# A sparse-expert stage whose first two experts get their token rows separately

## The reference

```
g_idx = argmax(h @ w_group + b_group)                  # one of 4 groups
el    = (h @ w_expert).reshape(N, 4, 8)[group] + b_expert
vals, idx = top_k(softmax(el), 2)                      # two experts of a token
for each expert e, over the rows of its tokens:
    y = (silu(x @ w1[e]) * (x @ w3[e])) @ w2[e]        # 1024 -> 512 -> 1024
out[token] += y * weight
```

## Time and profile before

| | us |
|---|---|
| median of 3 runs | 1858.24 (1854.73, 1858.24, 1860.97) |
| profiled execution, own time | 1859.26 |
| its span, first to last instruction | 1857.5 |
| PE busy | 1701.7 (92%) |
| mean granted TensorE clock | 0.978 of full |
| read from HBM | 329.75 MB |

### The profile page before, as it was taken

One profiled execution on the slowest core, in us unless ns is written; L12 is line 12 of the kernel. 1 busy time (PEld: TensorE's weight loads), 2 busy tenths in 40 slices (PEclk: granted clock), 3 DMA queues, 4 the chain that ended last, 5 costly groups with the idle time before them and its releaser, 6 DMA issues.

```text
span 1857.5 us, 24733 instructions
## 1 busy us (share of the span) xinstructions
PE 1701.7 (92%) x10405; PEld 1297.4 (70%) x10405; DVE 712.4 (38%) x1529; ACT 594.9 (32%) x1048; POOL 169.2 (9%) x128
## 2 busy tenths in 40 slices
PE   7999999997998877778889999997999899999998
PEld 5878766886564444444468966766788798888886
DVE  4355345454111111211135567555734532222223
ACT  3434354422011000000134456554624432222222
POOL 1000110221111111101001000011101000000221
PEclk9999899998999999999999999998999999999999
DMA  7512100358899999999994331012420232223201
GB/s 259 182 46 91 47 23 23 122 195 339 350 411 408 410 395 407 404 409 407 427 361 180 94 110 66 1 46 108 176 91 12 91 103 91 91 87 137 93 23 46
DMA packets 79580, 341.90 MB, mean 184 GB/s; under 512 B 8007, under 2 KB 15815, under 8 KB 66024
## 3 DMA queue, kind: packets, MB, share of 16 engines
q1 hardware_dynamic: 73192, 329.76, 46.0%
q0 software_dynamic: 5120, 8.40, 1.4%
q10 hardware_dynamic: 1152, 2.10, 0.3%
HBM read 329.75 MB, written 18.87 MB: 188 GB/s over the span
## 4 chain that ended last, share of the span: by engine, by line
PE 70%; DMA 19%; DVE 5%; ACT 4%; issue 2%; SPq 0%; POOL 0%; DVEq 0%; POOLq 0%; ACTq 0%
PE ps L553 66%; DMA arenaf<-in_w 14%; DMA arenaf<-in_mem 3%; DMA hf<-in_w_xkv 2%; PE ps L972 1%; PE ps L2881 1%; DMA ring<-in_w_in 1%; ACT splitr L629 1%; DVE arenaf L2963 1%; PE ps L807 1%; DVE splitr L618 0%; DVE arenaf L2981 0%; ACT arenaf L961 0%; PE ps L2059 0%; DVE xf L3259 0%
## 5 line engine op out<-in xcount | busy, mean ns | idle before, releaser
L553 PE MATMUL ps<-hr,splitr 128*128 128x512 f32 (+1 forms) x2784 | 579.1, 367 | 6.9 <-POOL hr L904 4.3
L553 PEld LDWEIGHTS ps<-hr,splitr 128*128 128x128 f32 x2784 | 476.5, 193 | 88.9 <-issue 5.1
L553 PE MATMUL ps<-splitr,hr 128*128 128x512 f32 (+1 forms) x1488 | 273.7, 343 | 2.2 <-DVE hr L1069 1.4
L553 PEld LDWEIGHTS ps<-splitr,hr 128*128 128x128 f32 x1488 | 234.2, 189 | 35.8 <-issue 2.0
L618 DVE TENSOR_TENSOR splitr<-ring,splitr 128x2048 fp32r<-128x2048 f32 x61 | 142.9, 2343 | 232.8 <-ACT splitr L629 232.6
L629 ACT CAST splitr<-ring 128x2048 fp32r<-128x2048 f32 x61 | 116.1, 1905 | 152.0 <-PE ps L553 142.7
L2096 DVE SCALAR_TENSOR_TENSOR tq<-ps,arenaf,tq 128x256 f32<-128x256 f32 x32 | 15.5, 484 | 268.8 <-PE ps L553 236.3
L2132 ACT COPY junk<-ps 64x512 f32<-64x512 f32 x32 | 18.5, 578 | 288.8 <-PE ps L553 288.8
L553 PE MATMUL ps<-arenaf,tq 128*64 128x512 f32 x336 | 81.5, 629 | 31.0 <-DMA arenaf<-in_w 31.0
L553 PE MATMUL ps<-arenaf 128*64 128x128 f32 (+7 forms) x784 | 103.0, 342 | 5.5 <-ACT arenaf L979 3.5
L618 DVE TENSOR_TENSOR splitr<-arenaf,splitr 128x2048 fp32r<-128x2048 f32 x27 | 62.2, 2303 | 104.9 <-ACT splitr L629 104.9
(11 more groups left out here) (395 smaller groups left out, 1926.0 us busy)
## 6 DMA issues: line engine op xcount, KB each, us to landing
ring<-in_w SPq DMA_DIRECT2D x22, 2048.0 KB, 43.1
arenaf<-in_w SPq DMA_DIRECT2D x22, 2048.0 KB
splitf<-in_w SPq DMA_DIRECT2D x21, 2048.0 KB, 44.0
hf<-in_w SPq DMA_DIRECT2D x20, 2048.0 KB, 44.5
ring<-in_w_in SPq DMA_DIRECT2D x11, 2048.0 KB, 9.6
otf<-in_w SPq DMA_DIRECT2D x11, 2048.0 KB
ring<-in_w_gate_up SPq DMA_DIRECT2D x7, 2048.0 KB, 7.9
arenaf<-in_w_in SPq DMA_DIRECT2D x4, 2048.0 KB
```

Of the source, the lines that this page charges most:

```text
L553: return te.matmul(out, lhsT, rhs, start=start, stop=stop)
```

## The change

The rows of pair 0 are no longer turned and gained for both experts at once. `pe_first_rows(e)` waits for the rows of expert e alone, and turns 64 rows (8 transposes that give 128x64) into two banks of its own. `ve_first_rows(e)` gains them. Expert 1's step stands behind `pe_up(0)`. Later pairs are as before. The events `("ert", 0, half)`, for which POOL's gathers 4 and 5 wait, now come with expert 1's transposes. `take` is called four times for pair 0 where it was called twice.

```diff
+            def pe_first_rows(e):
+                a = CAP * e
+                for half in range(2):
+                    ps = take("ert", 0, half, e)
+                    for w in pe_at(("rows", e)):
+                        te.wait_ge(*w)
+                    for k in range(4 * half, 4 * half + 4):
+                        c = CAP * (k % 4)
+                        it = te.transpose(ps[:, c:c + CAP], XG[0][a:a + CAP, k:1024:8], ident[a:a + CAP, a:a + CAP])
+                    it.then_inc(*pe_done("rows turned", ("ert", 0, half, e), *([("ert", 0, half)] if e else [])))
+
+            def ve_first_rows(e):
+                for half in range(2):
+                    ks = slice(4 * half, 4 * half + 4)
+                    gain = gain_moe[:, ks].rearrange("p (k o) -> p k o", o=1).broadcast_to([128, 4, CAP])
+                    for w in ve_at(("ert", 0, half, e), ("gain_moe",)):
+                        ve.wait_ge(*w)
+                    ve.tensor_tensor(XTF[:, ks, e, :], thirds(bank("ert", 0, half, e)[:, 0:4 * CAP], 4),
+                                     gain, ALU.mult).then_inc(
+                        *ve_done("rows gained", ("xgain", e, half, "first"), ("free", "ert", 0, half, e),
+                                 *([("xgain", 0, half)] if e else [])))
...
-                        for s in pe_at(("xgain", b // 2, k // 4)):
+                        for s in pe_at(("xgain", b // 2, k // 4) if b > 1 else ("xgain", b, k // 4, "first")):
...
             def pe_experts():
-                pe_rows(0)
+                pe_first_rows(0)
                 for b in range(33):
                     if b < 32:
                         pe_up(b)
+                    if b == 0:
+                        pe_first_rows(1)
...
             def ve_experts():
                 places_ = ve_extra_places()
-                ve_rows(0)
+                ve_first_rows(0)
                 for b in range(33):
                     if b < 32:
                         ve_hidden(b)
+                    if b == 0:
+                        ve_first_rows(1)
```

## The result

| | before | after |
|---|---|---|
| median, us | 1857.95 (6 runs, 1854.73 to 1860.97) | 1865.66 (6 runs, 1861.32 to 1870.72) |
| profiled execution: its own time, span | 1859.26, 1857.5 | 1861.32, 1859.4 |

The ratio is 1.0041, with a 95% interval of 1.0026 to 1.0055. The change made the kernel slower by 7.7 us, with an interval from 4.8 to 10.2. I had predicted +2.05 us. The sign was right, but 1865.66 lies above my range. The same kernel was timed once more later on beside the kernel before, and gave a ratio of 1.0029 (1.0017 to 1.0041), or 4.85 us.

What follows compares the result with a forecast made beforehand. Bound: PE's chain, and in the expert stage a full weight queue whose start follows expert 0's w1 product. Experts -0.95, bank wait +3.0, w_out_2 0: +2.05 on 1858.24 gives 1860.3 us, range 1854.5 to 1864.5.

Steps and rivals of the forecast that it cites:

- The experts: Expert stage: 1.7 us earlier start less 0.75 for gathers 4 and 5, so -0.95 us, between -2.9 and +0.2.
- The wait for gather 0 alone: Before expert 0's first product: PE no longer waits for gather 1, so its transposes start 1.3 us earlier.
- Half the rows: Before the first product: turning 64 rows saves 0.1 us, the smaller first gain 0.27.
- The clock in product 0: Expert 0's first product: the rise from 1.2 to 2.4 GHz follows the work, so the whole 1.7 us stays.
- rival 2: First product: the clock doesn't follow the work, gain only 0.85, experts -0.1, total +2.9, 1861.1 us; chance 0.20.
- rival 3: First product: the clock rises early, product ends 3.6 us earlier, experts -2.9, total +0.1, 1858.3 us; chance 0.09.
- Gathers 4 and 5: Expert stage: both gathers now run inside the full weight queue and cost 0.75 us, 1.07 by their share.
- The bank at the start of the attention: Sparse attention: first scores take mcol's bank and wait 2.6 us for ACT, clock 0.4 more; +3.0 (1.6 to 3.9).
- Rival 1: Start of the sparse attention: the stage swallows the new wait, which costs nothing; total -0.95, 1857.3 us; chance 0.16.
- Rival 4: First part of the attention: the clock stays at 1.2 GHz after the new gap; +4 more, 1864.3 us; chance 0.07.
- The product with w_out_2: Its 0.88 us wait goes, but PE then waits for head 3's squares: 0 us, bound -0.8.

Runs made afterwards that it cites:

- e1: Kernel before plus eight transposes of the identity in the middle of the expert stage; 1864.04 us against 1859.13, ratio 1.0029.
- e3: Kernel after with the bank ring's counter moved on by six at the end of PE's expert list; 1860.57 us against 1859.13 of before, ratio 1.0006.
- e11: Kernel before with the ring moved on by two after PE's expert list and eight identity transposes mid-stage; 1864.56 us against 1858.52, ratio 1.0036.
- e12: Kernel after, word for word, timed again beside the kernel before; 1863.37 us against 1858.52, ratio 1.0029.
- e9: Kernel before plus four transposes of the identity in the middle of the expert stage; 1864.06 us, timed only once.
- e10: Kernel before plus twelve transposes of the identity in the middle of the expert stage; 1863.05 us, timed only once.
- e4: Kernel before with the bank ring's counter moved on by two at the end of PE's expert list; 1861.51 us against 1859.13, ratio 1.0014.
- e5: Kernel before with gathers 4 and 5 also waiting for expert 0's turned hidden values, so as late as in after; 1859.66 us against 1858.47, ratio 1.0009.
- e2: Kernel after plus eight transposes of the identity in the middle of the expert stage; 1862.05 us, ratio 1.0019 to the kernel before.
- e6: Kernel after with the ring moved on by six after PE's expert list and eight identity transposes mid-stage; 1859.19 us against 1858.47 of before, ratio 1.0003.
- e7: e6 with expert 1's rows also turned and gained ahead of the first product; 1859.29 us against 1858.47 of before, ratio 1.0002.
- e8: e6 with gather 4 waiting only for expert 0's transposes and gather 5 for expert 1's; 1858.39 us against 1858.47 of before, ratio 1.0000.

## Why the prediction was wrong

**The step that failed is the list of what the change moves.** The prediction goes through PE's added work as time: eight transposes for 0.3 us that other work hides. As time this is right. What it leaves out is that they are also code. The prediction has no term for the branch, and this is the largest part of the miss: in the five profiles with the whole second pause (after, e1, e3, e11, e12) the stretch "branch" takes 13.56 us in the mean, in the eight without a second pause 10.70 (e9, with a part of the pause, is in neither). That is +2.9 us, and the two groups don't overlap: 12.61 to 14.21 against 9.65 to 11.35.

The pause of 3.73 us behind the branch could be read in the trace of before, and beside it the queue that serves it. It is q8, "instruction", with 84 packets and 1.38 MB in the whole kernel before, and 85 and 1.39 MB after. These are its rows among the DMA queues from 945 to 960 us, of before with three packets and then of e10 with two:

```profile
q8 instruction: 3, 0.05, 1.4%
```

```profile
q8 instruction: 2, 0.03, 0.9%
```

One packet is 16384 bytes. Away from the branch they are 12 to 43 us apart. Behind the branch the first two start at 951.0 and 954.2 before, and at 947.4 and 950.7 after: the second is not asked for until 3.2 or 3.3 us after the first. In the kernel after PE runs again at 949.97, uses up what the first block has left behind the branch's place (two matmuls), and waits until 953.62 for the second. The Trainium skill (Runtime: NRT & Kernel Launch, Instruction fetch mechanics) says that code is fetched ahead in blocks of 16 KiB or 256 instructions, and that a taken branch out of the blocks at hand forces a fetch before the engine goes on. The trace agrees with the size, and with a first pause that goes on 2.4 us beyond the landing of the weights in the kernel before. What I add from e1, e9 and e10 is that a second pause follows when the place where PE lands is near its block's end. From resuming to the end of the second pause are 3.1 to 3.65 us (0.48 + 2.63 in e11, 2.50 + 0.94 in e9, 0.70 + 2.95 in after), so work worth as much must lie between the place and the block's end. By e9's 5 matmuls behind 4 transposes the kernel before has about 9 there. At 0.35 to 0.50 us each (19 in 6.65 in after, 5 in 2.50 in e9) they are 3.2 to 4.5 us: estimated from these rows, the kernel before stood near the edge. The third packet bears this out. In the three kernels whose PE code has the length of before (before, e4, e5) it starts 4.3, 4.4 and 4.8 us after PE resumed, so PE went over a block's end shortly behind the branch there too, only without a pause. In the five with 24 or 32 instructions more (e2, e6, e7, e8, e10) none starts for another 23 us: they land behind that end.

**The experts: -0.95 forecast, about 0 measured.**
- The wait for gather 0 alone: 1.3 forecast, 1.37 measured. Right.
- Half the rows: I took 0.1 for the transposes by the row on weight loads, and 0.27 for the gain. Eight transposes of 64 rows took 1.15 us where those of 128 took 1.95, so the first gain starts 0.80 us behind the first transpose instead of 1.19: 0.39, not 0.1. The gain L2070 took 425 ns where it was 687 on average, so that term is right. Product 0 began 2.03 us earlier after gather 0, where I had 1.7: the end of my own bound (2.1), not my value. The weight load's price by its columns was no price for the whole transpose: in the rows the matmul part of each is 64x64 now, where it was 128x128, and took 314 ns where it took 421.
- The clock in product 0: I let the rise follow the work. In the profile of after product 0 took 6.37 us, and 0.76 of the 2.03 was lost again. So rival 2 is nearest to this profile: -1.27, with 0.85 by its own working. In e2, e3, e6 and e12 the clock rose earlier and the load went out 9.1 to 9.4 us after gather 0, up to 3.0 earlier than before, which is close to rival 3 (3.6). The same program did both (after and e12), so this term is not one number. Its row in e12:

```profile
462.47 4.89 PE L553 MATMUL ps<-ring,arenaf 128*64 128x256 f32 x32 [0.22 <-DVE arenaf L2070]
```

- Gathers 4 and 5: 0.75 forecast, with 1.07 as the upper bound, and 1.8 to 2.0 measured in e5 (by the end of its stage 1.5, against the mean of the six profiles with the order of before, below). The step "at 406 GB/s their bytes cost 0.74" failed. In the full queue the rate of all queues together falls from 418 to 346 GB/s for 6 us in e5 and to 322 in after, while the DMA engines are busy for 1.00 or more of the time. With 0.72 MB less moved in 60 us, they cost more than twice their 0.30 MB. By what mechanism is not shown. The share of 21.4% that I bounded it with the earlier trace rows was measured in a queue that was otherwise empty, and says nothing on what they do to other transfers.
- Net: from gather 0 to the end of the last product, 493.0, 492.1, 491.6, 492.7 and 491.8 us in the five profiles with the change's order (after, e2, e3, e6, e12), 492.2 in the mean; 492.3, 493.0, 491.4, 492.3, 492.3 and 493.0 in the six with the order of before (before, e1, e4, e9, e10, e11), 492.4 in the mean. Within a group they spread over up to 1.6 us. What the change bought here can't be told from nothing. One thing stays open: in e2, e3, e6 and e12 the first load went out 2.76 us earlier in the mean than in the six, and the stage ended only 0.32 earlier. The gathers account for 1.5 to 2.0 of the 2.4 us lost between, and where the rest went is not shown.

**The bank at the start of the attention: +3.0 forecast, +2.5 shown and about +3.3 with the clock.** The idle time is 2.59 less 0.06, so 2.53 (forecast 2.6) in all five kernels whose ring is shifted there (after, e2, e4, e11, e12), and in none of the others. The clock: from the first scores to the end of the product with `mqk` took 6.5 us in the mean of these five and 5.7 in the mean of the nine others, so 0.8 more instead of 0.4. But without the wait it lies between 4.0 and 7.0. The clock was low for 6.8 us in all five, and in the nine others for anything from no time (e5, e6) to 6.8 us. So this term hangs on when the clock fell and rose in each profile, and its 0.8 can't be told from chance. In the profile of after it cost 0.56 us against before, near the 0.4 forecast. Rival 1 (slack takes it up) fell: e3 and e4 lose and gain the idle time and nothing gives it back. Rival 4 (clock low for long) fell: the clock was back 4.6 us after PE went on.

**The product with w_out_2: 0 forecast, 0 measured.** From the end of the `mqk` product to the squares of head 3 are 204.4 us in after and 204.6 before. From there to the end of the program the five profiles with the shifted ring take 580.2 us in the mean and the nine others 581.0, so no other moved wait shows.

**The sum.** 2.9 + 3.3 - 0.1 + 0 = 6.1 us. The two timings give 7.7 (4.8 to 10.2) and 4.85 (ratio bounds 3.2 to 7.6), and both hold it. It is made of means over several profiles, in which single stretches scatter by up to 3 us. The single changes were timed too, and their intervals hold what the traces give for each: e1 2.8 to 8.2 us for a trace value of 2.9, e2 0.9 to 5.9 for 3.3, e3 -1.5 to 3.7 for 2.9, e4 0.0 to 5.2 for 3.3, and e11 4.1 to 9.3 for both together. Without the branch the loss would have been 3.2 us. The range was too narrow for another reason too: I closed it with terms that I had listed, and left no room for one I had not.

## What to carry to other kernels

Count added instructions as code where a taken branch follows: look at the "issue" pause behind the branch, at the packets of the instruction queue beside it, and at how much work stands between the place where the engine lands and the next block. Where banks, places or queues are handed out by a counter, one more call shifts all that follows; a line that completes the turn undoes it. A small gather that is moved into a full queue is priced by the fall of the whole rate there, not by its bytes.

## What the runs showed that I had not expected

- PE pauses for 3.5 to 4.65 us where it branches over unused code, in all fourteen profiles. In the thirteen in which the landing of the next weights can be read, 1.3 to 1.5 us of this would be a wait for them anyway. Up to 2.95 us come on top if PE lands near the end of a block of 16384 bytes. Four added transposes cost a pause of 0.94 us, eight one of 2.83, twelve none.
- Two gathers of 0.30 MB in a full queue cost 1.8 to 2.0 us, and one alone 1.0.
- The low stretch of the clock around the first product ended 6.6 to 7.1 us after gather 0 in four profiles with the change's early start and 9.9 to 10.4 us after it in the other ten, the earlier ones giving 1.4 to 1.7 us, of which by the end of the stage nothing is left that can be told from the scatter.
- Where the program is the same, its first 450 us differ by up to 6.6 us from one profile to the next (gather 0 at 453.0 to 459.7).
